# One group's end spread over the next group's slabs, and one split copy cut in halves, in the merge stage of a hybrid decoder layer

## What is computed

```python
o_a = (y_a.astype(x.dtype) * g) @ p['w_proj_a']
o_b = _moba(q_h, pos, blocks(k_all), blocks(v_all)).reshape(bsz, t_len, D_B) @ p['w_proj_b']
mix = jax.nn.sigmoid(gate_a) * o_a + jax.nn.sigmoid(gate_b) * o_b
x = x + gate1 * (mix @ p['w_out'])
```

## Time and profile before

| | |
|---|---|
| median of 3 runs | 2420.46 us (2417.21 to 2422.03) |
| the profiled execution | 2406.09 us |
| its span in the profile | 2404.3 us, mean granted TensorE clock 0.976 |
| TensorE busy | 2288.0 us (95% of the span), 19796 matmuls |
| VectorE, ScalarE busy | 1147.1 us (48%), 958.5 us (40%) |
| merge stage, from its first matmul to the first of `out` | 1289.37 to 1405.1 us |

### The profile page before, as it was taken

How to read it: one execution, slowest core, us unless ns; L and a number is a source line. 1 busy time by engine, 2 the same in 40 slices (tenths; PEclk the granted TensorE clock), 3 DMA queues, 4 the chain that set the end, 5 groups by cost and what they waited for, 6 DMA issues and landing times. The chain is left out here.

```text
span 2404.3 us, 49571 instructions
## 1 busy us (share of the span) xinstructions
PE 2288.0 (95%) x19796; PEld 2020.7 (84%) x19796; DVE 1147.1 (48%) x1901; ACT 958.5 (40%) x1413; POOL 107.3 (4%) x224
## 2 busy tenths in 40 slices
PE   6999899999999999978997999799999999999998
PEld 3889787888878888646666999799999999999998
DVE  3456635354353543525444555655454545544443
ACT  1433434334342433316552333354555554433333
POOL 0000010000100101000000000000000000000000
PEclk8999999999999999969998999999999999999999
DMA  9885566565666656577995445355555555555543
GB/s 320 275 305 155 147 187 182 180 184 176 189 185 186 193 169 192 170 231 251 388 388 200 155 156 167 97 167 166 166 165 164 164 164 164 166 166 164 161 149 117
DMA packets 326693, 461.22 MB, mean 192 GB/s; under 512 B 37337, under 2 KB 220395, under 8 KB 326075
## 3 DMA queue, kind: packets, MB, share of 16 engines
q1 hardware_dynamic: 318893, 450.42, 58.9%
q10 hardware_dynamic: 7634, 8.38, 1.0%
HBM read 442.86 MB, written 15.86 MB: 191 GB/s over the span
## 5 line engine op out<-in xcount | busy, mean ns | idle before, releaser
L953 ACT ACTIVATE whi<-raw 128x1024 fp32r<-128x1024 f32 (+1 forms) x512 | 526.2, 1028 | 912.0 <-PE ps L1966 885.9
L1966 PE MATMUL ps<-hhi,whi 128*128 128x288 f32 x2736 | 833.7, 305 | 12.1 <-DVE hlo L1453 6.4
L1966 PE MATMUL ps<-hhi,wlo 128*128 128x288 f32 x2736 | 809.8, 296 | 0.0
L1966 PE MATMUL ps<-hlo,whi 128*128 128x288 f32 x2736 | 809.2, 296 | 0.0
L1402 DVE TENSOR_TENSOR wlo<-raw,whi 128x1024 fp32r<-128x1024 f32 (+1 forms) x400 | 470.4, 1178 | 628.5 <-ACT whi L953 628.4
L1966 PEld LDWEIGHTS ps<-hhi,whi 128*128 128x128 f32 x2736 | 516.3, 189 | 75.3 <-issue 55.0
L1966 PEld LDWEIGHTS ps<-hlo,whi 128*128 128x128 f32 x2736 | 516.5, 189 | 1.2
L1966 PEld LDWEIGHTS ps<-hhi,wlo 128*128 128x128 f32 x2736 | 516.3, 189 | 0.0
L1966 PE MATMUL ps<-fhi,whi 128*128 128x288 f32 x704 | 208.3, 296 | 2.8 <-DVE wlo L1402 2.8
L1966 PE MATMUL ps<-fhi,wlo 128*128 128x288 f32 x704 | 208.0, 296 | 0.0
L1966 PE MATMUL ps<-flo,whi 128*128 128x288 f32 x704 | 207.6, 295 | 0.0
(11 more groups left out here) (392 smaller groups left out, 2764.3 us busy)
## 6 DMA issues: line engine op xcount, KB each, us to landing
raw<-in_w_up SPq DMA_DIRECT2D x352, 256.0 KB, 2.9
raw<-in_w_ada SPq DMA_DIRECT2D x128, 512.0 KB, 4.8
raw<-in_w_in SPq DMA_DIRECT2D x112, 512.0 KB, 4.5
raw<-in_w_down SPq DMA_DIRECT2D x88, 512.0 KB, 3.9
kpage<-in_cache_v SPq DMA_DIRECT2D x64, 512.0 KB, 5.9
raw<-in_w_in SPq DMA_DIRECT2D x72, 384.0 KB, 5.4
kpage<-in_cache_k SPq DMA_DIRECT2D x40, 512.0 KB, 5.4
ada_d<-in_w_ada SPq DMA_DIRECT2D x32, 512.0 KB, 4.9
```

The source lines that it names most:

```text
L953: return act.activation(o, i, ACT.Copy, **k)
L1966: return pe.matmul(out, lhsT, rhs, start=start, stop=stop, **k)
```

## The change

The four subtractions, four additions and the gating of branch B, which stood in one block behind slab 1, become three parts: gating behind slab 1, additions behind slab 2, subtractions behind slab 4. ScalarE's copies to `mhi` move from behind slab 2 to behind slab 3. Since `sga` is now read later, gating of branch A behind slab 5 gets a wait for the subtractions. The same spread is made over the slabs of the first `out` group. The split of `of` is made in two halves of four channel tiles: ScalarE does `hi` of slab 3 first, then the first half of `ohi`, `hi` of slab 4, and the second half; VectorE does `lo` of slab 3, the first half of `olo`, `lo` of slab 4, the second half. TensorE waits for the first half before slab 4 and for the second before slab 6; the counts of `merge_read` shift by one.

```diff
--- before.py
+++ after.py
@@ -1262,10 +1262,12 @@
             exps(NB - 1)
             outs(NB - 1)
 
-            for s in range(3):
+            for s in range(4):
                 hi("merge", G(0, None, 0), s)
             act.wait_ge(seq_copied, NB + 1)
-            copy(ohi[:, :, :], of[:, :, :]).then_inc(branch_hi, 1)
+            copy(ohi[:, 0:4, :], of[:, 0:4, :]).then_inc(branch_hi, 1)
+            hi("merge", G(0, None, 0), 4)
+            copy(ohi[:, 4:8, :], of[:, 4:8, :]).then_inc(branch_hi, 1)
 
 
             m0 = stages["merge"][0]
@@ -1276,13 +1278,13 @@
                     copy(mhi[:, bass.ds(g.at(4, q), 1), :].rearrange("p o t -> p (o t)"), sga[:, q, :]).then_inc(merged_hi_done, 1)
 
             def merge(g):
-                for s in range(3 if g.first else 0, 8):
+                for s in range(5 if g.first else 0, 8):
                     hi("merge", g, s)
-                    if s == 2 and not g.first:
+                    if s == 3 and not g.first:
                         merged_hi(g.prev())
 
             last_merge = singles(act, 4, merge)
-            plain("out", 1, out_added, {2: lambda: merged_hi(last_merge)})
+            plain("out", 1, out_added, {3: lambda: merged_hi(last_merge)})
             act.wait_ge(out_added, 4)
             norm_sums(1)
             norm_hi("up")
@@ -1854,8 +1856,11 @@
             out_rows(NB - 1)
             lo("merge", G(0, None, 0), 2)
             out_cols()
-            dve.wait_ge(branch_hi, KA + 1)
-            TTn(olo[:, :, :], of[:, :, :], ohi[:, :, :].bitcast(F32), ALU.subtract).then_inc(merge_read, 1)
+            for i in range(2):
+                lo("merge", G(0, None, 0), 3 + i)
+                dve.wait_ge(branch_hi, KA + i + 1)
+                h4 = slice(4 * i, 4 * i + 4)
+                TTn(olo[:, h4, :], of[:, h4, :], ohi[:, h4, :].bitcast(F32), ALU.subtract).then_inc(merge_read, 1)
 
 
             m0 = stages["merge"][0]
@@ -1866,23 +1871,32 @@
                 dve.wait_ge(gate_done, 8)
                 TTn(dst[:, :, :], gt[:, bass.ds(g.at(4, KD * ab), 4), :], ps[:, 4 * ab:4 * ab + 4, 0:T], ALU.mult).then_inc(merge_read, 1)
 
-            def merge_end(g):
-
-                gated(g, sgb, 1)
-                dve.wait_ge(merge_read, g.at(2, 3))
+            def merge_sum(g):
+
+                dve.wait_ge(merge_read, g.at(2, 4))
                 for q in range(4):
                     TTn(sga[:, q, :], sga[:, q, :], sgb[:, q, :], ALU.add).then_inc(merged, 1)
+
+            def merge_low(g):
+
                 for q in range(4):
                     dve.wait_ge(merged_hi_done, g.at(4, q + 1))
                     qc = bass.ds(g.at(4, q), 1)
                     TTn(fl(mlo[:, qc, :]), sga[:, q, :], fl(mhi[:, qc, :]).bitcast(F32), ALU.subtract).then_inc(merged_lo_done, 1)
 
             def merge(g):
-                for s in range(3 if g.first else 0, 8):
+                for s in range(5 if g.first else 0, 8):
                     lo("merge", g, s)
-                    if s == 1 and not g.first:
-                        merge_end(g.prev())
+                    if not g.first:
+                        if s == 1:
+                            gated(g.prev(), sgb, 1)
+                        if s == 2:
+                            merge_sum(g.prev())
+                        if s == 4:
+                            merge_low(g.prev())
                     if s == 5:
+                        if not g.first:
+                            dve.wait_ge(merged_lo_done, g.at(4))
                         gated(g, sga, 0)
 
             last_merge = singles(dve, 4, merge)
@@ -1913,7 +1927,8 @@
                 dve.wait_ge(ada_in_mod, ADA_G)
                 own(STT(gsc2[:, :, :], mod[:, 64:64 + KD, :], 1.0, bc(pcol("norm2_g").unsqueeze(2), [P, KD, NC]), ALU.add, ALU.mult))
 
-            residual("out", 32, out_added, {1: lambda: merge_end(last_merge), 3: scales2})
+            residual("out", 32, out_added, {1: lambda: gated(last_merge, sgb, 1), 2: lambda: merge_sum(last_merge), 3: scales2,
+                                                        4: lambda: merge_low(last_merge)})
             dve.wait_ge(out_added, 4)
             norm_h2("up")
             own(dve.memset(ext[:, :, 0:2], 0.0))
@@ -2589,12 +2604,12 @@
             for i in range(4):
                 g = G(0, None, i)
                 if i:
-                    pe.wait_ge(merge_read, 2 * i)
+                    pe.wait_ge(merge_read, 2 * i + 1)
                 products("merge", g, 0, 4, 0, yahi, yalo, between=None if i else last_outs)
-                pe.wait_ge(merge_read, 2 * i + 1)
-                products("merge", g, 4, 4, 4, ohi, olo)
-
-            pe.wait_ge(merge_read, 8)
+                pe.wait_ge(merge_read, 2 * i + 2 if i else 1)
+                products("merge", g, 4, 4, 4, ohi, olo, needs={} if i else {2: (merge_read, 2)})
+
+            pe.wait_ge(merge_read, 9)
             pe.wait_ge(merged_lo_done, 12)
             stage("out", mhi, mlo, out_added, 1, {6: (merged_lo_done, 16)})
             means(1, 3)
```

## The result

Ten timed runs of each kernel, medians: 2417.67 us before (2407.46 to 2422.03), 2401.19 us after (2393.28 to 2404.41). The ratio of after to before is 0.9944, 95% interval 0.9931 to 0.9957: 13.5 us less (10.4 to 16.7), where 13.2 were forecast. Against the base that the prediction used, 2420.46, this ratio gives 2406.9 us for a forecast of 2407.3.

The account below looks back on a forecast made before the run. TensorE, busy for 95% of the span, bounds the kernel, so time is won only where it waits or runs slowly. 7.09 + 6.12 = 13.2 us; 2420.5 - 13.2 = 2407.3 us, range 2402.5 to 2413.5.

Parts of the forecast that it names:

- the base: Whole kernel: timed median before, 2420.5 us, with its 14.4 us above the profiled execution taken as a constant.
- The ends: Four group ends, merge into `out`: spreading VectorE's block removes TensorE's waits and slower first matmuls, 1.77 us each, 7.09 together.
- 2.65 us behind a `lo` are free: VectorE in a slab: 1.95 us idle plus 0.7 us lead of the prepared slab cover added work.
- The idle times forecast: VectorE before the next `lo`: about 0.7 us left behind gating, 0.4 behind additions and subtractions.
- Rival D: Group ends: pieces stall as before, each waiting for another engine; only 6.1 us gained, 2414.4 us, chance 0.05.
- Group 0: First merge group: halved attention output removes the wait before slab 3, 3.39 us, and its low clock, 2.73; 6.12 together.
- The timetable: First merge group: slab 3 prepared by 1300.7 us, slab 4 by 1304.0, each 0.7 to 0.8 us before TensorE wants it.
- Rival B: First merge group: the wait goes but the clock falls all the same; gain 10.5 us, 2410.0 us, chance 0.12.
- the 2.73 us of the low clock: Slab 3 of the first merge group: 24 matmuls took 5.92 instead of 3.19 us at clock 0.50.
- Rival C: First merge group: halves don't help, the wait moves from slab 3 to slab 4; gain 7.1 us, 2413.4, chance 0.08.
- E: Behind the changed stages: an equal wait, such as for weights, turns up; nothing measurable, about 2420 us, chance 0.04.
- F: Start of the up stage: the clock's return falls otherwise and the kernel is slower, 2425.3 us or more, chance 0.03.

Follow-up runs that it names:

- the halves alone: Kernel before with only the attention output split in halves, group ends in one block as before: ratio to before 0.997, 6.06 us less on the stretch.
- the two variants with a middle dose: Changed kernel with half of `ohi` and `olo`, or a whole `ohi` but no `olo`, ahead of slab 3's preparation: 1.32 and 2.46 us more on the stretch.
- the ends alone: Changed kernel with the attention output split whole and in the old order again: ratio to before 0.9965, 7.15 us less on the stretch.
- the last: Changed kernel with the first four merge slabs loaded page by page and `hi` of slab 0 ahead of the last attention copy: ratio to before 0.9948.

## Why the prediction was right, and where it was off

**The ends.** Forecast 7.09 us; 7.15 alone, and the four periods from slab 2 of group 1 to slab 2 of the second `out` group take 101.77 us in the changed kernel, where 109.05 stood in the earlier trace rows: 7.28. The 0.19 us over the forecast are its undisturbed pace, which it took from `out` (25.49 us for 8 slabs); in the changed kernel a group of the merge takes 25.40. The step that carried it, that 2.65 us behind a `lo` are free, came out at 2.63. The idle times forecast (0.7 and 0.4) were 0.68 and 0.47. The extra wait ahead of gating of branch A costs nothing, as taken: gating starts right behind its `lo` at 1336.12. Rival D is out.

**Group 0.** Forecast 6.12 us; 6.06 alone. The timetable held to 0.2 us: slab 3 of the changed kernel follows slab 2 without a gap. Both terms are there, the wait and the low clock. Rival B, the clock falling anyway, is out: it did not in the changed kernel, nor in the halves alone or the two variants with a middle dose. The forecast took the 2.73 us of the low clock from one execution; the ends alone showed the same, but a price of this kind can differ, as said below. Rival C is out too, TensorE had no wait before slab 4. What the prediction gave to halves belongs mostly to the order, 5.57 of 6.28 us; it did not separate them. A small slip of reading: the first slice of the page's clock is at 8 as well as the 22nd, which touches no term.

**After the merge.** From the last `means` to the end of the span it is 885.6 us before and 885.5 after: no time was given back, so E and F are out. The clock behind the idle time at the up stage did vary, as the range allowed: from the last `means` to the up stage it takes 10.24 us before, 10.26 after, 9.41 to 10.57 in the variants.

**The step that was off** is the base: "no merge row explains that, so I take it as a constant", said of the 14.4 us between the timed median and the profiled execution. It is no constant but scatter, and in the profiled executions it lies in what runs before the merge. The kernels with the ends only and with the halves only were profiled 0.8 and 0.2 us above their timed medians, the changed kernel 4.9 below. `hi` of merge slab 2 starts between 1294.4 and 1312.1 us in the ten profiled executions, 17.7 us apart, while the time from the last `means` to the end lies between 885.2 and 886.8. The profiled execution before, 2406.09 us, lies near the low end of that kernel's runs, which took from 2403.91 to 2422.03. So a bound of 2.4 us for the median was too small: 1.3 us of the miss below the range come from it, and not from the change. Of the scatter, about 4 us are there by 280 us (the first matmul of the small low-rank products starts between 279.1 and 283.4) and 11 us by 1080 (the first rotation of queries, 1080.0 to 1091.2, over the first six of the kernels above). It goes with the clock: among the 23 runs of the kernel before that were timed beside the first variants, the mean granted clock is 0.979 in the shortest (2403.91 us) and 0.970 to 0.972 in the four above 2420 us. Why TensorE is longer at the lower level in some runs is not shown.

The Trainium skill, "TensorE: Matmul & The Clock Gate", Part 1, says that one and the same kernel shows different numbers of slow matmuls from run to run. Here the code up to the merge is the same in all kernels but the last, and the traces agree, at a price of about 1 us: from its first matmul to the `hi` of slab 2 that waits for it, slab 0 took 5.05 us in the kernel before and 5.95 in the changed one, behind the same 3.44 us of idle time; the other executions with 3.44 us lie between 5.04 and 5.93.

What the Trainium skill, "VectorE: DVE Perf Modes", says in its section on the TRN2 errata on the fixed cost of an instruction spoke against the halves. It had no price here: halves and whole differ by 0.14 us on VectorE, which fell into the cover, and the whole `olo` cost 0.71 us more by standing in one piece before slab 4.

## What to carry to other kernels

In a pipeline where TensorE waits for slabs that two engines prepare, work on these engines is free up to their idle time and the lead of the prepared slab together (here 1.95 + 0.7 us), and costs what exceeds it at every place; so cut a block into parts below that size, and put each waiting part a slab behind what it waits for. Look first at what is queued behind a long instruction: letting a ready slab go ahead gave 5.6 us, cutting the instruction 0.7. And when an edit is worth less than the scatter of runs, read a stretch between two events around it, with an end that no idle time of TensorE stands ahead of.

## What the runs showed that I had not expected

Behind a stop of TensorE, even one of 0.24 us, the first matmul takes 0.20 to 0.24 us to the next start instead of 0.13, at the full clock; these 0.07 to 0.11 us are no part of the idle time in the profile. A late start of up to 0.16 us or so is no idle time there at all, as lengths of matmuls are modelled. And eight equal matmuls of `means` took from 2.88 to 4.18 us in ten executions of nearly the same code, by where the clock fell.
